# Row-wise norm in the front, memory keys and values inside the projection: one change to a decoder step kernel

## The reference, cut to what matters

```
def rms_norm(x, g):
    y = x * rsqrt(mean(x * x, axis=-1) + 1e-6)
    return y * g
u    = rms_norm(x, norm_mix_g) @ w_in          # first 1792 columns: time mixing
xs   = u + (u_prev - u) * shift_mu             # u_prev: the row before
mem  = rms_norm(mem_prompt, norm_mem_g)        # 256 rows
p_mem_k = rms_norm(heads(mem @ w_mk), mem_k_g) # 4 heads x 128
p_mem_v = mem @ w_mv
```

## Time and profile before

| | us |
|---|---|
| median of 3 runs | 2996.5 (2993.27 to 2996.67) |
| span of the profiled execution | 2988.9 |
| its own time beside the span | not listed |
| first projection matmul starts | 115.43 |
| last projection matmul starts | 280.42 |

### The profile page before, as it was taken

The page is one execution under the profiler, slowest core; times in us unless marked ns, Lnnn a source line. Parts: engine busy times, 40 slices in busy tenths (PEclk is TensorE's granted clock), DMA queues, the critical chain, the costliest instruction groups (busy, mean ns, idle before and its releaser), DMA issues. The chain is left out here.

```text
span 2988.9 us, 49084 instructions
## 1 busy us (share of the span) xinstructions
PE 2687.8 (90%) x21514; PEld 2403.6 (80%) x21514; DVE 1156.3 (39%) x2020; ACT 796.6 (27%) x1246; POOL 163.0 (5%) x215
## 2 busy tenths in 40 slices
PE   5898588887898689987799999999889999999998
PEld 4798488873897455653599999998679999999998
DVE  4433644425142566634422232443453222222223
ACT  3222322211113344432222121222433212222212
POOL 1000221210211000011000000000000000000000
PEclk8999799987999599998899999999999999999999
DMA  5610100004511000027721111502211111111111
GB/s 167 236 46 15 17 3 3 3 4 145 121 44 47 18 1 1 1 106 248 278 55 45 46 51 43 146 8 75 81 36 43 43 50 43 50 48 45 43 50 66
DMA packets 178933, 192.09 MB, mean 64 GB/s; under 512 B 18214, under 2 KB 162897, under 8 KB 173624
## 3 DMA queue, kind: packets, MB, share of 16 engines
q1 hardware_dynamic: 168665, 127.05, 14.5%
q0 software_dynamic: 9888, 61.87, 5.9%
q10 hardware_dynamic: 168, 0.04, 0.0%
HBM read 165.28 MB, written 28.00 MB: 65 GB/s over the span
## 5 line engine op out<-in xcount | busy, mean ns | idle before, releaser
L3398 PE MATMUL ps<-ff_hidden_high,ff_high 128*128 128x352 f32 x768 | 247.7, 323 | 0.0
L3399 PE MATMUL ps<-ff_hidden_low,ff_high 128*128 128x352 f32 x768 | 246.7, 321 | 0.0
L3400 PE MATMUL ps<-ff_hidden_high,ff_low 128*128 128x352 f32 x768 | 246.4, 321 | 0.0
L586 PE MATMUL ps<-xf_h,ff_high 128*128 128x352 f32 x720 | 232.3, 323 | 2.1 <-DVE ff_low L575 2.1
L587 PE MATMUL ps<-xf_l,ff_high 128*128 128x352 f32 x720 | 230.8, 321 | 0.0
L588 PE MATMUL ps<-xf_h,ff_low 128*128 128x352 f32 x720 | 230.6, 320 | 0.0
L2998 PE MATMUL ps<-xn_h,me_gate_w_high 128*128 128x352 f32 x576 | 187.1, 325 | 4.9 <-DVE me_gate_w_low L3064 4.9
L2999 PE MATMUL ps<-xn_l,me_gate_w_high 128*128 128x352 f32 x576 | 185.7, 322 | 0.0
L3000 PE MATMUL ps<-xn_h,me_gate_w_low 128*128 128x352 f32 x576 | 185.5, 322 | 0.0
L3507 DVE TENSOR_TENSOR x<-x,ps 128x1056 f32<-128x1056 f32 x64 | 80.3, 1254 | 224.9 <-PE ps L3400 224.9
L3501 DVE TENSOR_TENSOR ff_hidden_low<-ff_act,ff_hidden_high 128x1056 fp32r<-128x1056 f32 x32 | 40.3, 1258 | 306.9 <-ACT ff_hidden_high L3473 306.9
(11 more groups left out here) (702 smaller groups left out, 6367.8 us busy)
## 6 DMA issues: line engine op xcount, KB each, us to landing
ff_raw<-in_w_ff SPq DMA_DIRECT2D x64, 512.0 KB, 4.0
me_gate_w_raw<-in_w_in SPq DMA_DIRECT2D x23, 512.0 KB
pj_raw<-in_w_in SPq DMA_DIRECT2D x13, 512.0 KB, 4.3
xn_high<-xn_h POOLq DMA_DIRECT2D x1, 4224.0 KB, 12.1
xn_low<-xn_l POOLq DMA_DIRECT2D x1, 4224.0 KB, 23.6
xn_h<-xn_high POOLq DMA_DIRECT2D x1, 4224.0 KB, 16.2
xn_l<-xn_low POOLq DMA_DIRECT2D x1, 4224.0 KB, 26.5
xn_h<-xn_high SPq DMA_DIRECT2D x1, 4224.0 KB, 13.1
```

The lines of the kernel that those rows point to most:

```text
L586: e.matmul(o, W.hi[:, z, k, :], rh[:, k, n], start=k == ks[0], stop=False)
L3398: e.matmul(o, W.hi[:, u % NSPL, 2 * k + z, :], hh[:, r, ns], start=k == 0, stop=False)
L3399: e.matmul(o, W.hi[:, u % NSPL, 2 * k + z, :], hl[:, r, ns], start=False, stop=False)
L3400: mm = e.matmul(o, W.lo[:, u % NSPL, 2 * k + z, :], hh[:, r, ns], start=False, stop=k == GB - 1)
```

## The change

In the front, the sum of squares is taken per token row, before the transpose: ACT squares the row tile as it lies in its slot and accumulates along the free axis, one number per token. Mean, root and reciprocal work on columns of a 128x9 tile in two parts (tiles 0 to 3; tiles 4 to 8). PE spreads each column over all partitions, in PSUM, with a matmul of the broadcast column against the identity. DVE multiplies from there, in halves of 512 and 544 tokens; the normed x has a tile of its own, so no chunk waits for another's low part. Memory work leaves the front. The parameter rows come in 23 DMAs, 16 on ACT and 7 on SP, `shift_mu` in 6 instead of 15. Of the sheet only the identity comes first, the rest behind the x tiles.

In the projection stage, PE turns the memory rows behind blocks 0 and 1 (banks 6 and 7), multiplies one weight piece behind each of the blocks 2 to 5 and 7 to 10, and turns the keys behind block 6. The memory norm is per row too (ACT squares with accumulation, DVE scales rows of 128x1024), the gain goes in as the scale of the copy behind the transpose: eight ACT and eight DVE operations of 128x128 for each of the blocks 0 and 1 in place of the wide ones. The weight pieces have one slot, the four stores of keys and values are issued by ACT behind blocks 6, 7 and 10, and DVE waits ahead of four blocks of `xs` whose room the memory tiles use. SP loads the small tables of the next stage earlier, but the one-hot table behind the last piece. The diff below is cut: semaphore increments and repeated waits are left out, several short lines are drawn into one, and a few lines only name what stands there.

```diff
 SP, front
-    e.dma_start(K.cst[:, :], K.d["sheet"][:, 0:RESIDENT])
+    e.dma_start(K.cst[:, 0:P], K.d["sheet"][:, 0:P])
...
+    for name, cnt in params[6:]: load_param(e, name, cnt)
     for i in range(3, NTI + 1):
         e.wait_ge(s_xt, i - 2)
+        e.wait_ge(s_sq, i - 2)
         tile(i)
+    e.dma_start(K.cst[:, P:RESIDENT], K.d["sheet"][:, P:RESIDENT])
+    e.dma_start(mem_rows[:, :, :], K.d["mem_prompt"][0]...)
...
 ACT, front
+    def squares(i):
+        e.wait_ge(s_x[i % 3], 16 * (i // 3 + 1))
+        e.activation(spare[0:n, i % 2, :], xin[0:n, i % 3, :], ACT.Square, accum_out=ss[0:n, i:i + 1])
+    for i in range(4): squares(i); copy(i)
+    squares(4); root(0); copy(4)
+    for i in range(5, NTI): squares(i); copy(i)
+    squares(NTI); copy(NTI); root(1); high(0); high(1)
...
 PE, front
+    def spread(z):
+        e.wait_ge(s_inv, z + 1)
+        for i in range(4 * z, 4 * z + 4):
+            mm = e.matmul(K.ps[:, 4 + z, P * (i % 4):P * (i % 4) + P], ss[:, i:i + 1].to_broadcast([P, P]), ident)
+    turn(0..3); transposes of parameter and shift rows; turn(4); spread(0); turn(5..8); spread(1)
...
 DVE, front
+    copy(0..3); mean(0); copy(4); invert(0)
+    parameter and shift copies
+    copy(5); norm(0, range(4)); copy(6); norm(0, range(4, KD))
+    copy(7); copy(8); mean(1); invert(1); norm(1, range(KD)); low(0); low(1)
...
 SP, projection
+    load_piece(0)
     for m in range(W.pre, count):
         load_block(m)
+        if 6 <= m <= 10: load_piece(m - 5)      # waits for the low part of the piece before
+        if 12 <= m <= 13: load_piece(m - 6)
+    e.wait_ge(s_p, 8)
+    e.dma_start(lora.oh[:, :], K.d["onehot"])
...
 PE, projection
     for m in range(count):
         product(e, K, W, m, xh, xl, 3 * (m % 2), range(KD))
+        if m in TURNED: turn_rows(m)             # (0, 1)
+        if m in BEHIND: piece(BEHIND.index(m))   # (2, 3, 4, 5, 7, 8, 9, 10)
+        if m == KEYS: turn_keys()                # 6; waits for the key norm
...
 ACT, projection, behind the copies of block m and high_block(m + 2)
+        if m in TURNED: 2 x (4 copies of 128x128 with scale, after turn_rows)
+        if m == TURNED[1]: weight_high(0)
+        if m in BEHIND:
+            if p % 2 == 1: take(p // 2)
+            if p < 7: weight_high(p + 1)
+            if p == 3: e.wait_ge(s_kss, 1); Sqrt of the key sums
...
 DVE, projection, behind the token shift of block m
+        if m in TURNED: 2 x (4 low parts of 128x128)
+        if m == TURNED[1]: weight_low(0)
+        if m in BEHIND:
+            if p < 7: weight_low(p + 1)
+            if p == 3: key_norm()
+        if m == KEYS: copy of the turned keys
```

More of the change, by code:

```diff
@@ L189, in stage_front @@
[L189 to L194, removed]
@@ L195, in stage_front @@
-        s_out, s_scr = K.out_sem("mk_stored"), K.sem("fm_scratch_stored")
+        s_set, s_sq, s_var, s_root, s_inv, s_sp, s_nrm, s_hi = (K.sem("fx_" + x) for x in (
+            "sums_cleared", "squared", "mean", "root", "inverted", "spread", "normed", "high"))
         ntok = lambda i: P if i < NTI else TS
-        chunk = lambda c: slice(NW * c, NW * c + NW)
-        tiles_of = lambda c: -(-(NW * c + NW) // P)
         half = lambda i, z: K.ps[:, 2 * (i % 2) + z, :].rearrange("p (k n) -> p k n", k=4)[:, :, 0:ntok(i)]
-        pbank = lambda u, i: 6 + i if u % 2 == 0 else 2 + i
+        parts = (slice(0, HALF), slice(HALF, T))
@@ new lines, in stage_front, with load_param @@
+        columns = (slice(0, 4), slice(4, NTI + 1))
+        params = [(name, cnt) for name, cnt in PARAMS if name not in ("nsa_q_g", "kg_cmp", "shift_mu")]
+        def load_param(e, name, cnt):
+            src = K.d[name]
+            if name == "rwkv_rk":
+                src = src.rearrange("a (c h) d -> (a c) (h d)", c=cnt)
+            else:
+                src = src.rearrange("a (c p) -> (a c) p", p=P)
+            e.dma_start(prow[PCOL[name]:PCOL[name] + cnt, :], src).then_inc(s_prow, 16)
@@ L216, in _ @@
                 e.wait_ge(s_xt, i - 2)
+                e.wait_ge(s_sq, i - 2)
                 tile(i)
[L218 to L227, removed]
+            e.dma_start(K.cst[:, P:RESIDENT], K.d["sheet"][:, P:RESIDENT]).then_inc(s_rest, 16)
+            e.dma_start(mem_rows[:, :, :], K.d["mem_prompt"][0].rearrange("(i p) d -> p i d", p=P)).then_inc(s_mem_rows, 16)
             for m in range(ahead.nraw):
@@ L306, in _, with root, high @@
-            for i in range(6):
+            def root(z):
+                e.wait_ge(s_var, z + 1)
+                e.activation(ss[:, columns[z]], ss[:, columns[z]], ACT.Sqrt).then_inc(s_root, 1)
+            def high(z):
+                e.wait_ge(s_nrm, z + 1)
+                e.activation(xh[:, :, parts[z]], xn[:, :, parts[z]], ACT.Copy).then_inc(s_hi, 1)
+            e.wait_ge(s_set, 1)
+            for i in range(4):
+                squares(i)
                 copy(i)
-            squares(0)
@@ L309, in _ @@
-            squares(1)
+            squares(4)
             root(0)
-            for i in range(6, NTI + 1):
+            copy(4)
+            for i in range(5, NTI):
+                squares(i)
                 copy(i)
+            squares(NTI)
+            copy(NTI)
+            root(1)
             high(0)
[L314 to L318, removed]
@@ L319, in _ @@
-            high(1)
[L320 to L333, removed]
@@ L465, in _, with low @@
+            def low(z):
+                e.wait_ge(s_hi, z + 1)
+                e.tensor_tensor(xl[:, :, parts[z]], xn[:, :, parts[z]], xh[:, :, parts[z]].bitcast(F32), ALU.subtract)
+            e.memset(ss[:, :], 1.0).then_inc(s_set, 1)
+            for i in range(4):
                 copy(i)
             mean(0)
-            norm(0)
-            for i in range(6, NTI + 1):
-                copy(i)
+            copy(4)
+            invert(0)
+            e.wait_ge(s_par, 1)
+            e.tensor_copy(K.par[:, 0:NPAR], K.ps[:, 7, 0:NPAR])
@@ L470, in _ @@
+            copy(7)
+            copy(8)
             mean(1)
[L471 to L474 removed]
+            invert(1)
+            norm(1, range(KD)).then_inc(s_nrm, 1)
             low(0)
[L476 to L478 removed]
@@ L634, in _ @@
             high_block(e, W, 0, landed[0])
             high_block(e, W, 1, landed[1])
+            e.wait_ge(s_mem_rows, 16)
+            for i in range(2):
+                if i >= 1:
+                    e.wait_ge(s_msq, i)
+                e.activation(M.squares[:, :], M.rows[:, i, :], ACT.Square, accum_out=M.rstd[:, i:i + 1]).then_inc(s_msq, 1)
+            e.wait_ge(s_mvar, 1)
+            e.activation(M.rstd[:, :], M.rstd[:, :], ACT.Sqrt).then_inc(s_mroot, 1)
             for m in range(count):
@@ L658, in _ @@
             e.memset(u[:, 1, 0:1], 0.0)
+            e.wait_ge(s_msq, 2)
+            e.tensor_scalar(M.rstd[:, :], M.rstd[:, :], 1.0 / D, RMS_EPS, ALU.mult, ALU.add).then_inc(s_mvar, 1)
+            e.wait_ge(s_mroot, 1)
+            e.reciprocal(M.rstd[:, :], M.rstd[:, :])
+            e.drain()
+            for i in range(2):
+                mm = e.tensor_scalar(M.rows[:, i, :], M.rows[:, i, :], M.rstd[:, i:i + 1], None, ALU.mult)
+            mm.then_inc(s_mnrm, 1)
             for m in range(count):
@@ L4123, in build @@
         K.turn = {}
-        K.n_prow = sum(2 if n in ("nsa_q_g", "kg_cmp") else 15 if n == "shift_mu" else 1 for n, _ in PARAMS)
+        K.n_prow = sum(2 if n in ("nsa_q_g", "kg_cmp") else 6 if n == "shift_mu" else 1 for n, _ in PARAMS)
         K.live = []
```

440 lines of the change are left out of this document (234 added, 206 removed).

## The result

| | before | after |
|---|---|---|
| median, us | 2995.4 (4 runs, 2993.27 to 2996.67) | 2945.78 (4 runs, 2943.41 to 2949.5) |
| profiled execution: time, span | not shown, 2988.9 | 2947.55, 2945.3 |

What follows compares the result with a forecast made beforehand. A chain of hand-overs bounds the front, PE the projection. -64.6 + 26.1 + 0.6 + 0.3 = -37.6 us takes the span from 2988.9 to 2951.3; 7.6 more gives 2959 us, own range 2953 to 2964, 8 in 10 within 2948 to 2971.

Steps and rivals of the forecast that it cites:

- First product: End of the front: first projection product starts at 50.8 us, bounds 45 and 59, 64.6 us earlier than 115.43.
- The spread: Norm in the front: PE spreads a half's 8 to 10 records over partitions in 1.8 to 2.2 us.
- Projection: Projection stage: memory work adds 26.1 us on PE, plus 0.6 of idling at block 5 and 0.3 for switching.
- Sum up to the last product: Front and projection together: -64.6 + 26.1 + 0.6 + 0.3 = -37.6 us.
- The median of the runs is 2996.5, 7.6 above the span, and I keep that distance.: Final step: 7.6 us from span to median kept, taking the forecast span of 2951.3 to 2959 us.
- Everything after 280 us is untouched by the diff and I let it shift as it stands.: Behind the projection: all later work keeps its length, 2708 us after the last product, and only shifts.
- The wrong-if condition: Behind the projection: forecast wrong if the stretch after the last product is over 3 us off 2708 us.
- x tiles late: Front: x tiles land late, first product at 56 to 61 us, kernel 2964 to 2969 us; chance 0.18.
- PE waiting at memory steps: Projection: PE waits 1 us at each of ten memory steps, kernel 2969 us; chance 0.12.
- VectorE as pace-maker: Projection: VectorE takes PE's place, kernel slower than before if each of ten memory steps grows over 3.8 us; chance 0.03.
- the front was not shorter than forecast: Front: rival that DVE never waits and ends at 42, first product at 45, kernel 2953 us; chance 0.07.
- The rival on waits that bring half clock: Projection: in the slower-than-before rival, waits drop PE to its cold rate, 1.7 us more each, 3016 at 4 us; chance 0.03.

Runs made afterwards that it cites:

- before_newparams: The kernel before with only the parameter rows loaded as in the kernel after, 16 transfers by ACT and 7 by SP: 2985.54 us, ratio 0.9974.

## Why the prediction was wrong

What it said of the changed work held. First product 51.9 (50.8, bounds 45 to 59). Norm of the second half 6.5 us (6.4), low parts 9.0 (9.1), accumulating squares 1.06 plus 0.18 for the read of the sum (1.1), ACT free at 6.4 and past its table load at 7.8 (6.1, 7.4). The spread was off: five products in 2.6 us, at a granted clock of 0.50, so that the second norm began at 33.7 instead of 32.2. Projection 190.4 against 165.0: +25.5 (26.1 + 0.6 + 0.3 = 27.0); without memory in it 26.1 us less. Key wait 0.2 (0.6). Sum up to the last product -38.1 (-37.6); the first product 1.1 us late and the projection 1.5 us short of the forecast offset each other, so the sum is nearer than its terms.

Two steps failed, both outside the diff.

*"The median of the runs is 2996.5, 7.6 above the span, and I keep that distance."* The distance from span to time of one execution is 2.2 us in nearly every run. The rest was the draw of executions: the profiled one took 2988.9 + 2.2 = 2991.1, the three others had a median of 2996.5, and that kernel's executions in all rounds have medians from 2991.4 to 2995.4, a mean of 2992.9 and spread over 2981 to 3005. So the profiled one was 1.8 us under the mean and the median of three 3.6 over it. An offset between two different executions is noise, not a constant. It put the forecast 5.4 us too high.

*"Everything after 280 us is untouched by the diff and I let it shift as it stands."* The wrong-if condition, a stretch behind the last product over 3 us away from 2708, came true: it was 2703 in the first profile. Untouched instructions don't keep their length here, since stretches of half clock fall in them differently, in the loop by the count of slow pairs. That was 5.5 us in this profile. Over three profiles of each the loop's part is 2.9 us; over all executions the untouched part is some 7, of which the other 4 are not placed. Alone, this step puts the forecast 8 us too high: the mean of 2992.9 less 37.6 is 2955, and after's is 2947.0.

With 0.5 us in the front and projection and 1.8 us by which the profile of after lies above its median, these are the 13.2 us between 2959 and 2945.8. The mean of after's nine plain executions is 2947.0 us, 12 below the forecast. The first profile of after, with only one slow pair, was a lucky one for the loop: the next two had two and three.

Rivals: x tiles late, PE waiting at memory steps and VectorE as pace-maker did not occur; the front was not shorter than forecast. The rival on waits that bring half clock stood in the right mechanism and the wrong stage: not in the projection, where PE has no gap, but in the loop behind it.

What stays open: what fixes the places of half clock for a given kernel. The kernel before has the same loop in three profiles and the kernel after three different ones. Open too are some 4 us of the gain behind the loop; and before_newparams is 8 us faster with the same loop and first product.

## What to carry to other kernels

Put a forecast on the span of one execution and the median of many only together with the spread: take the offset from runs that show both, and where PE's gaps bring half clock widen the range by what such a stage can vary (here 7 us in one loop, 278.6 to 285.7, and 6 in one stage). When judging an edit, compare where its last changed instruction falls, not the end of the kernel. A gap of 2 to 4 us on PE ahead of a busy stretch is worth a try with idle products, measured in the kernel at hand: eight small products a chunk brought 14 us in the kernel before and nothing clear of noise in the kernel after (2946.33 against 2948.99).

## What the runs showed of the hardware

- Fifteen waits of up to 2.5 us (22.0 us in all) stand in a loop of 286 us in the kernel before. With the largest filled, the loop took 274.6 and its stage 319.9 instead of 327.4 us: 7.5 us were the price.
- Two chunks of that loop, the same matmuls, take 37.9 us at granted clocks of 0.92 and 1.00, or 40.7 at 0.84 and 0.91.
- One wait of 4.1 us has two outcomes, some 162.3 or 168.0 us for the same stage, seven and eight times, by when the clock falls.
- A first mask 3.0 us later was given back by such a loop in the kernel before (282.8 instead of 285.7 us).
- An accumulating square of 128x1024 on ACT took 1.06 us, and 0.18 more for the read of the sum.
- The x tiles moved at 300 GB/s over the first 40 us (DMA busy 0.89), where the kernel before had 239 over 50 us: so 239 was no limit of the transfers.
